# Single indexer heads, and an attention order planned by batches of two groups, in a two-layer streaming encoder

## The chip, the cores and the metric

The kernel runs on one core of a Trainium2 chip. The metric is device time in microseconds (us), the median of three runs. The engines run their own instruction streams and meet at semaphores: TensorE (PE in the rows, with its weight loads as PEld), VectorE (DVE), ScalarE (ACT), GpSimd (POOL) and SyncE (SP), whose queue issues the DMAs. Every engine works through its stream in order.

## The reference, cut to what matters

Two layers over a prompt of 1024 tokens and a sample of 32 tokens that sees a cache of 1024 rows. All arithmetic is in float32.

```python
h = rms_norm(x, g_norm[l]);  a_q, a_k, a_v, i_q, i_k, i_w, b_q, b_k, b_v, m_q, gate = project(h, w_in[l], pos)
# the indexer: 4 heads of 64, one score for every query and key
dots  = einsum('bqhd,bld->bqhl', iq, ik_all)
score = einsum('bqh,bqhl->bql', iw, relu(dots)) * IDX_SCALE      # -inf where the key's chunk is later
_, idx = top_k(score, 256)
# A: softmax attention of 8 heads (2 kv heads) over the chosen keys; B: 4 heads, sliding window, sink;
# M: 4 heads over 256 memory tokens
xp = xp + (concat(o_a, o_b, o_m) * silu(gate)) @ w_out[l]
```

## The kernel before, in words

Tokens are worked in nine tiles: eight of 128 prompt rows (t = 0 to 7) and the sample (t = 8, 32 rows). Tile t has 128 (t + 1) keys, the sample 1056. Keys are not gathered: the top 256 are found as a threshold per query, and a mask in `bias` (0 or -3e38) is added to the scores of group A. Tiles 0 and 1 have at most 256 keys and need no search.

`plan()` writes one list, `STEPS`, and each engine walks it and does its own part of each step. So the list is the order of work on every engine. A layer has these stages:

- **Key stage.** For each tile `SQUARE`, `KEYS` (projection into two score banks), `NORM` (the normed rows of tile t+2 turned by TensorE, copied by VectorE), `KEYS_T` (keys turned), `CACHE` (cache rows turned), `ROPE` (on VectorE). Between them stand the four `INDEX` steps of tile t-2, in the order `KEYS`, INDEX, `NORM`, INDEX, `KEYS_T`, INDEX, `CACHE`, INDEX, `ROPE`. The INDEX steps of tile 7 follow in a row, and those of the sample stand between `QUERIES` 0, `MEM` 0 and `MEM` 1.
- **INDEX before.** `("INDEX", t, hp, c)` is a pair of heads hp and a chunk c of up to 512 keys. TensorE does two matmuls (L837), one head each, on rows 0 to 63 and 64 to 127 of the array. ScalarE does two `Relu` activations (L1053), VectorE a `tensor_scalar` (L1320) or `scalar_tensor_tensor` (L1322) for each head. `index_relu` has two buffers, and step u waits for VectorE to be done with step u-2. A tile has 2 steps up to 512 keys and 4 above, the sample 6.
- **Search.** `TOPK`: 32 rounds on VectorE and ScalarE, beside `QUERIES` and `GATE` on TensorE.
- **Attention.** `attention_steps()` writes it. The items are (t, B), (t, A, kv 0), (t, M), (t, A, kv 1) for each t. `QK` gives scores: an item of kind A takes 2 steps up to 512 keys and 4 above, each a chunk for two heads. VectorE adds the mask, keeps the maximum (L1354) and frees the score buffer. ScalarE then takes the exponentials (L1099) when both chunks are there. For kind B VectorE does the same with the window mask (L1383, exponentials L1113). For kind M (and B of the sample) VectorE only takes the maximum (L1379) and ScalarE reads the score banks itself (L1113), so the banks are held until the exponentials are done.
- `PT` turns a group of four 128x128 blocks of probabilities into one of two `turn_ps` banks (L731). ScalarE (L1124) or VectorE (L1444) copies it to `prob_t`: `copied_by_dve(a)` gives VectorE two groups in five. `PV` multiplies with the values (L915, L927). `MIX` (L1460, VectorE) multiplies with the gate.
- Groups are held until there are two. Then both `PT` are written, then both `PV` of the two groups before. Score steps of item i+2 are dealt out over the groups of item i, each before the `PT` of its group, so ScalarE meets exponentials ahead of the copies of the same pair.
- `OUT` t-1, halves 0 and 1 (L746, 16 instructions each) stand before two groups of tile t (`OUT_AT`). Beside each stands a half of the mask of tile t+1: `need_of_tile` and `mask_tile` (L1210 to L1237). `ADD` (L1474) adds the residual and frees the banks.
- `SCALE` takes the reciprocal of the sums, SP writes it to memory and reads it back spread over partitions (`norm_turn`), and `GATE_SCALE` on GpSimd (L1154) puts it into the gate, which `MIX` waits for. Tile 0 divides its probabilities instead (`DIVIDE`, L1434) before they are turned.

`score_ps` has two buffers of two banks, and `KEYS`, `INDEX`, `QUERIES`, `MEM`, `GATE`, `QK`, `OUT` and `EXTRA` use them by turns. The order around tile 6 before, where each line is one pair of `PT`:

```
QK 6A1.0                 PT 6B.1  PT 6A0.0   PV 5A1.5 MIX PV 6B.0   SCALE 6
OUT 5.0 MASK ADD  QK 6A1.1   PT 6A0.1 PT 6A0.2   PV 6B.1  PV 6A0.0
QK 6A1.2                 PT 6A0.3 PT 6A0.4   PV 6A0.1 PV 6A0.2
```

## Time and profile before

| | |
|---|---|
| median of three runs | 1604.13 us (1602.92 to 1609.43) |
| the profiled execution | 1599.02 us |
| its span | 1597.2 us |
| TensorE's mean granted clock | 0.949 |

The span runs from the first to the last record of the profile. The 1.8 us between it and the profiled execution's time lie around it. Layer 0 takes 0 to 786 us and layer 1 786 to 1566 us, with the same pattern: the attention is 431 to 785 us and 1213 to 1566 us. A row of a timeline gives the start, the duration, the engine, the line, and in brackets how long the engine was idle before it and what ended the wait. Every float32 matmul shows as two instructions.

### The profile page before, as it was taken

Reading aid. Unit: us, or ns where it says so; the run is one execution under the profiler, and the core shown is the slowest. Engines: PE = TensorE matmul, PEld = TensorE weight load, DVE = VectorE, ACT = ScalarE, POOL = GpSimd, SP = SyncE. Lnnn points to the kernel's source line nnn. Section 1 sums busy time; section 2 is a strip of 40 time slices with the busy share of each in tenths; the row PEclk is TensorE's granted clock in tenths of the full one; section 3 lists DMA queues with packets and bytes.
Section 4 is the critical chain, followed back from the end, with each engine's and each line's share of the span. In section 5 each row is a group of like instructions: output and inputs, shape, how many; then the busy total and the mean of one; then the engine's idle time right before and its main releaser. Section 6 shows DMA issues by size and latency. Waiting matters only on the chain. (4 is left out here: it accounts for less than half of the span.)

```text
span 1597.2 us, 19488 instructions
## 1 busy us (share of the span) xinstructions
PE 1400.2 (88%) x6364; PEld 778.1 (49%) x6364; DVE 920.6 (58%) x2527; ACT 657.4 (41%) x1667; POOL 155.9 (10%) x187
## 2 busy tenths in 40 slices
PE   5988799999889999988599887999997999998881
PEld 3444356666545444444344343666664444544450
DVE  1444636887656677655133446488775557676533
ACT  1123526776634433333111334377655333344332
POOL 1100013300001000000011001132000001000003
PEclk9999999999989999999689998999998999999976
DMA  6100410123132312111241004003124222111106
GB/s 200 53 25 21 156 47 1 45 88 94 67 88 73 80 53 54 26 35 29 62 160 52 25 18 161 27 0 119 35 86 133 54 57 57 54 47 53 34 4 247
DMA packets 117960, 108.58 MB, mean 68 GB/s; under 512 B 52368, under 2 KB 90992, under 8 KB 117872
## 3 DMA queue, kind: packets, MB, share of 16 engines
q1 hardware_dynamic: 117872, 107.45, 22.1%
q8 instruction: 51, 0.84, 0.2%
q14 instruction: 37, 0.30, 0.1%
HBM read 81.76 MB, written 25.76 MB: 67 GB/s over the span
## 5 line engine op out<-in xcount | busy, mean ns | idle before, releaser
L746 PE MATMUL score_ps<-w_slot,hT 128*128 128x512 f32 (+2 forms) x1024 | 391.9, 542 | 12.5 <-ACT prob_bm L1053 7.6
L746 PEld LDWEIGHTS score_ps<-w_slot,hT 128*128 128x128 f32 x1024 | 197.7, 196 | 193.3 <-issue 187.3
L746 PE MATMUL score_ps<-w_slot,work 128*128 128x512 f32 x512 | 234.6, 612 | 5.5 <-issue 5.4
L1099 ACT ACTIVATE hT<-hT,neg_top 128x128 f32<-128x128 f32 (+8 forms) x144 | 116.8, 812 | 288.0 <-DVE neg_top L1372 287.8
L1253 DVE TENSOR_SCALAR_CACHE_REDUCE work<-bias,trial 128x384 f32<-128x384 f32 (+3 forms) x256 | 226.1, 883 | 6.9
L969 ACT ACTIVATE work<-bias,neg_trial 128x768 bf16<-128x768 f32 (+2 forms) x192 | 198.4, 1043 | 67.3 <-DVE neg_trial L1249 67.3
L746 PEld LDWEIGHTS score_ps<-w_slot,work 128*128 128x128 f32 x512 | 97.5, 196 | 129.8 <-issue 129.6
L817 PE MATMUL score_ps<-hT,w_slot 128*128 128x352 f32 x448 | 135.2, 460 | 1.4 <-ACT gate_raw L1083 1.4
L731 PE MATMUL turn_ps<-ident,hT 128*128 128x128 f32 (+1 forms) x720 | 98.9, 277 | 27.6 <-ACT work L1124 17.2
L1154 POOL TENSOR_TENSOR work<-work,norm_sb 128x512 f32<-128x512 f32 (+1 forms) x32 | 38.9, 1216 | 855.7 <-DMA norm_sb<-norm_scratch 855.7
L871 PE MATMUL score_ps<-akT,query_mem 64*128 64x512 f32 (+4 forms) x448 | 103.1, 547 | 9.4 <-ACT prob_bm L1113 6.5
L731 PEld LDWEIGHTS turn_ps<-ident,hT 128*128 128x128 f32 (+1 forms) x720 | 74.5, 147 | 74.0 <-issue 33.2
L817 PEld LDWEIGHTS score_ps<-hT,w_slot 128*128 128x128 f32 x448 | 84.8, 190 | 48.4 <-issue 1.7
L1354 DVE CUSTOM_DVE_ANT_0 hT<-score_ps,bias 128x512 f32<-128x512 f32 (+4 forms) x144 | 80.8, 598 | 42.9 <-PE score_ps L871 42.4
L1021 ACT COPY work<-score_ps 128x64 f32<-128x64 f32 (+2 forms) x112 | 20.5, 300 | 179.0 <-PE score_ps L746 179.0
L1124 ACT COPY work<-turn_ps 128x512 f32<-128x512 f32 (+1 forms) x102 | 56.6, 570 | 81.9 <-PE turn_ps L731 81.9
L1474 DVE TENSOR_TENSOR gate_raw<-score_ps,gate_raw 128x512 f32<-128x512 f32 x32 | 22.1, 692 | 118.1 <-PE score_ps L746 118.1
L1320 DVE TENSOR_SCALAR bias<-prob_bm,iw_sign 128x512 f32<-128x512 f32 (+5 forms) x26 | 12.9, 496 | 125.8 <-ACT prob_bm L1053 125.5
L927 PE MATMUL out_a_ps<-work,a_v_sb 128*64 128x256 f32 (+1 forms) x560 | 73.7, 382 | 0.0
L731 PE MATMUL turn_ps<-ident,prob_bm 128*128 128x128 f32 (+2 forms) x280 | 43.3, 286 | 34.3 <-ACT work L1124 24.5
L731 PE MATMUL turn_ps<-ident,work 128*128 128x128 f32 (+1 forms) x284 | 44.3, 292 | 32.8 <-DVE hT L1285 14.9
L1322 DVE SCALAR_TENSOR_TENSOR bias<-prob_bm,iw_sign,bias 128x512 f32<-128x512 f32 (+5 forms) x78 | 51.6, 661 | 29.1 <-ACT prob_bm L1053 26.9
(179 smaller groups left out, 1768.2 us busy)
## 6 DMA issues: line engine op xcount, KB each, us to landing
w_slot<-in_w_in_dram SPq DMA_DIRECT2D x8, 2048.0 KB, 10.3
gate_raw<-in_x_prompt_dram SPq DMA_DIRECT2D x16, 512.0 KB, 3.7
work<-gate_scratch SPq DMA_DIRECT2D x16, 512.0 KB, 4.7
x_scratch<-gate_raw SPq DMA_DIRECT2D x16, 512.0 KB, 4.6
gate_raw<-x_scratch SPq DMA_DIRECT2D x16, 512.0 KB, 3.5
norm_sb<-norm_scratch SPq DMA_DIRECT2D x56, 128.0 KB, 4.1
gate_scratch<-gate_raw SPq DMA_DIRECT2D x16, 264.0 KB, 3.1
gate_scratch<-gate_raw SPq DMA_DIRECT2D x8, 528.0 KB, 2.6
```

The lines of the kernel that those rows point to most:

```text
L731: last = nc.tensor.transpose(flat[0:c, pitch * i:pitch * i + r], src, ident[0:r, 0:r])
L746: last = nc.tensor.matmul(out[:, 0:cols], lhs(k), w[:, k, 0:cols], start=(k == 0), stop=(k == KD - 1))
L817: last = nc.tensor.matmul(o, w[:, k, :], hT_v[:, k, THIRD * c:THIRD * (c + 1)], start=(k == 0), stop=(k == KD - 1))
L871: last = nc.tensor.matmul(out[0:r, 512 * u:512 * u + w], aqT[half, head, t * P:t * P + r], akT[half, k0:k0 + w], start=True, stop=True)
L927: last = nc.tensor.matmul(out[HD * u:HD * (u + 1)], v, p.rearrange("p (h n) -> p h n", h=2), start=first and m == 0, stop=final and m == l ...
L969: ins = nc.scalar.activation(signs[c][0:r, 0:NKEYS[t]], bias[0:r, KEY_OFF[t]:KEY_OFF[t + 1]], ACT.Sign, bias=neg_trial[0:r, i:i + 1], accu ...
L1099: ins = nc.scalar.activation(p, p, ACT.Exp, bias=neg, scale=SM_SCALE, accum_out=sums[t % 2][0:r, col:col + 1])
L1124: nc.scalar.copy(prob_t[a % 4][0:w, 0:n], bank.rearrange("p k n -> p (k n)")[0:w, 0:n]).then_inc(free, 1)
L1154: nc.gpsimd.tensor_tensor(gate_sb[t % 2][:, k, 0:r], gate_sb[t % 2][:, k, 0:r], norm_sb[:, k, 0:r], ALU.mult).then_inc(gate_scaled[bm], 1)
L1253: linked(nc.vector.tensor_scalar(tie_a[0:ROWS[t], 0:NKEYS[t]], scored(c), value[0:ROWS[t], c:c + 1], None, ALU.is_ge, ALU.add, accum_out=c ...
L1322: ins = nc.vector.scalar_tensor_tensor(out=s, in0=rl, scalar=sign, in1=s, op0=ALU.mult, op1=ALU.add)
L1354: ins = nc.vector.tensor_tensor_reduce(prob[0:r, head + at:head + at + w], ps[0:r, 512 * u:512 * u + w], bias[0:r, k0 + at:k0 + at + w], 1 ...
```

## The change

- **Single heads.** `("INDEX", t, h)` is one head over all its keys. TensorE does its chunks one after the other on the same 64 rows of the array, ScalarE one `Relu` over up to 1024 columns, VectorE one operation over all keys. Every tile has 4 steps. The sample's last 32 keys go to `out_bm_ps` with a semaphore of their own, and its relu buffers are `relu_sb`, for which ScalarE waits that the keys are stored. VectorE's own wait for that before the search goes.
- **Batches.** The groups are paired once and for all. Score steps of item i go one to a batch (several where it is crowded), so that the last stands two batches before the item's first `PT`. In a batch stand: `OUT`, parts of the mask, `ADD`, the score steps, both `PT`, the `PV` of the batch before, then the `SCALE` of the scores of the batch before.
- **Copies in front.** ScalarE walks `scalar_order(STEPS)`: exponentials that read SBUF come after the `PT` copies of their batch. Those that read the score banks (M, and B of the sample) stay ahead of the copies.
- **Masks in parts.** The mask of a tile is nine parts; 0 to 2 (only for the tiles of `BY_ACT`: 5, 6 and 7) can stand in batches without an `OUT`, 3 to 5 with or before the first half of `OUT`, 6 to 8 with or before the second.

The new order around tile 6, at the start of the attention and at its end:

```
QK 6A0.3   PT 5A1.3 PT 5A1.4   MIX PV PV
MASK.0     PT 5A1.5 PT 6B.0    MIX PV PV
MASK.1 QK 6A1.0              PT 6B.1  PT 6A0.0   PV 5A1.5 MIX PV 6B.0
OUT 5.0 MASK.2-5 ADD QK 6A1.1    PT 6A0.1 PT 6A0.2   PV PV
QK 6M QK 6A1.2               PT 6A0.3 PT 6A0.4   PV PV
start: EXTRA QK 0A0.0 0A0.1 0M 0A1.0 0A1.1  DIVIDE 0B PT 0B  DIVIDE 0A0 PT 0A0  QK 1B 1A0.0 1A0.1  DIVIDE 0M ...
end:   QK 8M 8A1.0-3  PT 8B.1 PT 8A0.0  PV MIX 7.0 PV / OUT 7.0 ADD  PT PT PV PV SCALE 8.1 SCALE 8.0 / ...
```

```diff
@@ -48,7 +48,6 @@
 SEARCH_STEPS = 32
 
 
...
 CACHE_GROUPS = 6
...
+def batches():
+
+    groups = [(i, g) for i in range(len(ITEMS)) for g in range(len(groups_of(ITEMS[i])))]
+    return [groups[k:k + 2] for k in range(0, len(groups), 2)]
...
+def mask_parts(t):
+
+    return list(range(0 if t in BY_ACT else 3, 9))
...
+def scores_by_batch(first, last):
+
+
+    at, early = [[] for _ in range(last[len(ITEMS) - 1] + 1)], []
+    for i in range(1, len(ITEMS)):
+        units, before = score_steps(i), buffer_of(i)[1]
+        if before is None and first[i] < 2:
+            early += units
+            continue
+        low = 0 if before is None else last[before] + 1
+        for n, unit in enumerate(units):
+            at[max(low, first[i] - 1 - len(units) + n)].append(unit)
+    return early, at
+
+
 def attention_steps():
...
+    plan = batches()
+    first, last = {}, {}
+    for b, groups in enumerate(plan):
+        for i, _ in groups:
+            first.setdefault(i, b)
+            last[i] = b
+    early, scores = scores_by_batch(first, last)
...
+    out, masks = [[] for _ in plan], [[] for _ in plan]
+    for t in range(1, TILES):
+        here, prev = ITEMS.index((t, "B", 0)), ITEMS.index((t - 1, "A", 1))
+        out0 = last[prev] + 2
+        out[out0].append(("OUT", t - 1, 0))
+        if t == SMP:
+            continue
+        ahead = next(b for b in range(len(plan)) if ("QK", ITEMS.index((t + 1, "A", 0)), 0) in scores[b])
+        out1 = max(out0, min(ahead, first[ITEMS.index((t, "M", 0))]))
+        out[out1].append(("OUT", t - 1, 1))
+        if t + 1 in SEARCHED:
+            for k in mask_parts(t + 1):
+                b = first[here] + k if k < 3 else out0 if k < 6 else out1
+                masks[min(b, out0, ahead) if k < 6 else min(b, ahead)].append(("MASK", SEARCHED.index(t + 1), k))
...
+    def products(groups):
+        made = []
+        for i, g in groups:
+            t, kind, kv = ITEMS[i]
+            made.append(("PV", i, g))
+            if g == len(groups_of(ITEMS[i])) - 1 and kind == "M":
+                made.append(("MIX", t, 1))
+            elif g == len(groups_of(ITEMS[i])) - 1 and (kind, kv) == ("A", 1):
+                made.append(("MIX", t, 0))
+        return made
+
+    steps, waiting, mixes = [("EXTRA",)] + early, [], []
+    for b, groups in enumerate(plan):
+        steps += out[b] + masks[b] + [("ADD",) + s[1:] for s in out[b]]
+        steps += scores[b]
+        for i, g in groups:
+            if ITEMS[i][0] == 0 and g == 0:
                 steps.append(("DIVIDE", i))
-            held.append(("PT", i, g))
-            if len(held) == 2 or (i, g) == last_group:
-                steps += held
-                mixes, last_mixes = last_mixes, []
-                steps += mixes
...
+            steps.append(("PT", i, g))
+
+
+        steps += mixes
+        mixes = []
+        for s in products(plan[b - 1]) if b else []:
+            (mixes if s[0] == "MIX" and s[2] else steps).append(s)
+        steps += waiting
+        waiting = [d for q in scores[b] for d in divisors(q)]
+    steps += mixes + waiting + products(plan[-1])
     return steps + [s for t, c in ((NT - 1, 1), (SMP, 0)) for s in (("OUT", t, c), ("ADD", t, c))]
...
+def scalar_order(steps):
+
+
+    order, scores, last = [], [], None
+    for s in steps:
+        if last == "PT" != s[0]:
+            order += scores
+            scores = []
+        if s[0] == "QK" and s[1] and not reads_scores(ITEMS[s[1]]):
+            scores.append(s)
+        else:
+            order.append(s)
+        last = s[0]
+    return order + scores
...
-        index = index_steps(t - 2) if t - 2 in SEARCHED else []
+        index = [("INDEX", t - 2, h) for h in range(IDX_HEADS) if t - 2 in SEARCHED]
...
-    steps += index_steps(NT - 1) + [("KEYS_T", SMP)]
-
-    last = index_steps(SMP)
...
+    steps += [("INDEX", NT - 1, h) for h in range(IDX_HEADS)] + [("KEYS_T", SMP)]
+
     for h, filler in enumerate([("QUERIES", 0), ("MEM", 0), ("MEM", 1)]):
-        steps += [filler] + last[2 * h:2 * h + 2]
-    assert len(last) == 6
+        steps += [filler, ("INDEX", SMP, h)]
+    steps.append(("INDEX", SMP, IDX_HEADS - 1))
...
                         elif kind == "INDEX":
-                            t, hp, c = step[1:]
-                            if (hp, c) == (0, 0):
+                            t, h = step[1:]
+                            if h == 0:
                                 turn_taken(pe, ("KEYS_T", t), 0)
                                 if t == SMP:
                                     turn_taken(pe, ("KEYS_T", t), 1)
-                            r, k0 = ROWS[t], (0 if t < SMP else SEQ) + 512 * c
-                            w = min(512, NKEYS[t] - 512 * c)
+                            r, half, k0 = ROWS[t], HD * (h % 2), 0 if t < SMP else SEQ
                             out = score_buffer(step)
-                            for u in range(2):
-                                half = slice(HD * u, HD * (u + 1))
-                                last = nc.tensor.matmul(out[0:r, 512 * u:512 * u + w],
-                                                        iqT[half, hp, t * P:t * P + r],
-                                                        ikT[half, k0:k0 + w], start=True, stop=True)
+                            q = iqT[half:half + HD, h // 2, t * P:t * P + r]
+                            for c in range(0, NKEYS[t], 512):
+                                w = min(512, NKEYS[t] - c)
+                                if c < 1024:
+                                    o = out[0:r, c:c + w]
+                                else:
+                                    if h:
...
 
                     counted = 0
-                    for step in STEPS:
...
                             nc.scalar.copy(bkT[:, k0:k0 + r], bank[:, 2, 0:r]).then_inc(free, 1)
                         elif kind == "INDEX":
-                            t, hp, c = step[1:]
-                            r, w, u = ROWS[t], min(512, NKEYS[t] - 512 * c), INDEX_STEPS.index(step)
+                            t, h = step[1:]
+                            r, n = ROWS[t], NKEYS[t]
+                            u = IDX_HEADS * SEARCHED.index(t) + h
                             ps, free = scores(step)
                             act.wait_ge(iw_done, t + 1)
+                            relu = (index_relu if t < SMP else relu_sb)[u % 2]
+                            if (t, h) == (SMP, 0):
+                                for b in range(2):
+                                    act.wait_ge(kv_stored[b], 16 * kv_dmas(b, TILES))
                             if u >= 2:
-                                act.wait_ge(score_added, 2 * (u - 1))
-                            for k in range(2):
-                                at = slice(512 * k, 512 * k + w)
-                                ins = nc.scalar.activation(index_relu[u % 2][0:r, at], ps[0:r, at], ACT.Relu,
-                                                           scale=iw_abs[0:r, t, 2 * hp + k:2 * hp + k + 1])
+                                act.wait_ge(score_added, u - 1)
+                            scale = iw_abs[0:r, t, h:h + 1]
+                            ins = nc.scalar.activation(relu[0:r, 0:min(n, 1024)], ps[0:r, 0:min(n, 1024)],
+                                                       ACT.Relu, scale=scale)
                             ins.then_inc(free, 1)
+                            if n > 1024:
+                                ins = nc.scalar.activation(relu[0:r, 1024:n], out_bm_ps[0:r, 0, 0:n - 1024],
+                                                           ACT.Relu, scale=scale)
+                                ins.then_inc(extra_free, 1)
                         elif kind == "QUERIES":
                             t = step[1]
...
 
-                    def need_of_tile(i):
+                    def mask_part(i, k):
...
+                        low, part = least[0:r, i:i + 1], margin[0:r, i:i + 1]
+                        if k == 0:
                             link(nc.vector.tensor_scalar(rank, x, v, None, ALU.is_gt, ALU.add,
                                                          accum_out=count[0:r, i:i + 1]))
+                        elif k == 1:
                             link(nc.vector.tensor_scalar(equal, x, v, 3.4e38, ALU.is_le, ALU.mult))
+                        elif k == 2:
...
                             link(nc.vector.tensor_scalar(part, part, -1.0, 1.0, ALU.mult, ALU.add))
                             link(nc.vector.tensor_tensor(v, v, part, ALU.mult))
                             link(nc.vector.tensor_tensor(v, v, low, ALU.add))
-                        link(nc.vector.tensor_scalar(rank, x, v, None, ALU.is_gt, ALU.add,
-                                                     accum_out=count[0:r, i:i + 1]))
-                        link(nc.vector.tensor_scalar(need[0:r, i:i + 1], count[0:r, i:i + 1], -1.0, float(TOPK),
-                                                     ALU.mult, ALU.add))
-
-                    def mask_tile(i):
...
                             nc.vector.tensor_copy(ikT[:, k0:k0 + r], bank[:, 3, 0:r]).then_inc(free, 1)
                         elif kind == "INDEX":
-                            t, hp, c = step[1:]
-                            r, n, u = ROWS[t], NKEYS[t], INDEX_STEPS.index(step)
-                            w = min(512, n - 512 * c)
-                            scores_taken(dve, step)
-                            s = bias[0:r, KEY_OFF[t] + 512 * c:KEY_OFF[t] + 512 * c + w]
-                            for k in range(2):
-                                rl = index_relu[u % 2][0:r, 512 * k:512 * k + w]
-                                sign = iw_sign[0:r, t, 2 * hp + k:2 * hp + k + 1]
-                                if (hp, k) == (0, 0):
-                                    ins = nc.vector.tensor_scalar(s, rl, sign, None, ALU.mult)
-                                else:
-                                    ins = nc.vector.scalar_tensor_tensor(out=s, in0=rl, scalar=sign, in1=s,
-                                                                         op0=ALU.mult, op1=ALU.add)
-                                signal(ins, score_added, 2 * u + k + 1)
-                            if hp == IDX_HEADS // 2 - 1 and 512 * c + w == n and t < SMP:
-
-                                link(nc.vector.memset(s[0:CHUNK, w - CHUNK:w], NEG))
+                            t, h = step[1:]
+                            r, n = ROWS[t], NKEYS[t]
+                            u = IDX_HEADS * SEARCHED.index(t) + h
+                            if n > 1024:
+                                dve.wait_ge(extra_free, h + 1)
+                            else:
+                                scores_taken(dve, step)
+                            s, rl = bias[0:r, KEY_OFF[t]:KEY_OFF[t] + n], (index_relu if t < SMP else relu_sb)[u % 2][0:r, 0:n]
+                            sign = iw_sign[0:r, t, h:h + 1]
+                            if h == 0:
...
+                            else:
+                                ins = nc.vector.scalar_tensor_tensor(out=s, in0=rl, scalar=sign, in1=s,
...
                         elif kind == "QK":
                             i, j = step[1:]
```

## Rows read from the trace of the kernel before

**Rows 1.** The page: busy time by engine, and the granted clock over 40 slices.

```profile
PE 1400.2 (88%) x6364; PEld 778.1 (49%) x6364; DVE 920.6 (58%) x2527; ACT 657.4 (41%) x1667; POOL 155.9 (10%) x187
...
PEclk9999999999989999999689998999998999999976
```

**Rows 2.** Busy time (count) by engine, clock, DMA by stretch: key stage, attention.

```profile
90.00:208.00 118.00, 97.39 (x375) 47.04 (x374) 57.82 (x123) 39.92 (x116) 4.02 (x8) 0.91 0.22 73
431.00:786.00 355.00, 311.94 (x1768) 165.69 (x1767) 208.41 (x592) 130.35 (x359) 19.87 (x16) 0.95 0.21 56
```

**Rows 3.** Waits by PE, 461 to 745: waiting line, releaser, total, times, longest.

```profile
PE turn_ps L731 <- ACT work L1124: 19.3, 14, 2.5
...
PE turn_ps L731 <- ACT prob_t L1124: 1.9, 2, 0.9
```

**Rows 4.** Busy time of the same stretch.

```profile
461.00:745.00 284.00, 259.60 (x1376) 134.16 (x1375) 181.37 (x479) 106.73 (x286) 18.96 (x14) 0.99 0.19 50
```

**Rows 5.** Timeline, attention, around one wait: start, duration, engine, operation.

```profile
634.63 0.60 PE L731 MATMUL turn_ps<-ident,prob_bm 128*128 128x128 f32 x4
634.67 1.22 DVE L1379 TENSOR_REDUCE top<-score_ps 128x4 f32<-128x1024 f32 x1
...
638.20 0.47 ACT L1113 ACTIVATE prob_bm<-score_ps,neg_top 128x256 f32<-128x256 f32 x1
...
638.65 1.07 ACT L1124 COPY work<-turn_ps 128x512 f32<-128x512 f32 x2
...
639.29 0.66 PE L731 MATMUL turn_ps<-ident,prob_bm 128*128 128x128 f32 x4 [1.99 <-ACT work L1124]
```

**Rows 6.** Timeline, start of attention.

```profile
438.07 0.49 PE L871 MATMUL score_ps<-akT,query_mem 64*128 64x128 f32 x4 [3.27 <-ACT prob_bm L1113]
...
441.46 2.08 PE L884 MATMUL score_ps<-bkT,bqT 64*128 64x256 f32 x8
...
447.02 1.97 PE L731 MATMUL turn_ps<-ident,prob_bm 128*128 128x128 f32 x8 [3.48 <-DVE prob_bm L1434]
```

**Rows 7.** Timeline, key stage, one tile of 512 keys.

```profile
119.89 1.13 PE L837 MATMUL score_ps<-query_mem 64*128 64x512 f32 x4
...
120.95 1.10 PE L731 MATMUL turn_ps<-ident,gate_raw 128*128 128x128 f32 x8
...
122.82 0.49 DVE L1320 TENSOR_SCALAR bias<-prob_bm,iw_sign 128x512 f32<-128x512 f32 x1 [12.86 <-ACT prob_bm L1053]
...
123.34 0.75 DVE L1322 SCALAR_TENSOR_TENSOR bias<-prob_bm,iw_sign,bias 128x512 f32<-128x512 f32 x1
...
124.97 1.05 PE L731 MATMUL turn_ps<-ident,work 128*128 128x128 f32 x7 [1.86 <-DVE hT L1285]
```

**Rows 8.** As rows 2, gaps between projections (INDEX of tiles 2, 3, 4, 5, 6+7, sample).

```profile
97.63:105.93 8.30, 4.75 (x28) 3.10 (x28) 5.37 (x12) 4.17 (x16) 0.00 (x0) 0.91 0.00 0
119.89:128.60 8.71, 4.91 (x28) 2.83 (x28) 5.57 (x12) 4.59 (x16) 0.00 (x0) 0.98 0.00 0
143.17:152.38 9.21, 6.77 (x37) 3.61 (x36) 3.31 (x10) 5.36 (x19) 0.00 (x0) 0.81 0.00 0
165.51:174.27 8.76, 6.19 (x37) 3.23 (x37) 4.32 (x10) 5.63 (x19) 0.00 (x0) 1.00 0.00 0
177.86:198.93 21.07, 12.82 (x59) 5.53 (x56) 17.60 (x37) 11.79 (x29) 0.00 (x0) 0.86 0.77 265
211.62:232.57 20.95, 19.21 (x94) 13.34 (x93) 6.22 (x9) 7.58 (x19) 4.39 (x4) 1.00 0.07 25
```

**Rows 9.** Timeline, PE: the first projection of queries.

```profile
198.93 12.76 PE L746 MATMUL score_ps<-w_slot,hT 128*128 128x512 f32 x32 [3.00 <-ACT prob_bm L1053]
```

**Rows 10.** Timeline: an output projection of 16 instructions.

```profile
523.46 7.10 PE L746 MATMUL score_ps<-w_slot,work 128*128 128x512 f32 x16 [0.41 <-issue]
```

**Rows 11.** Timeline, end of attention: the round trip of the divisors.

```profile
745.16 0.19 DVE L1414 RECIPROCAL inv_sum<-sums 32x8 f32<-32x8 f32 x1
...
753.66 0.45 POOL L1154 TENSOR_TENSOR work<-work,norm_sb 128x128 f32<-128x128 f32 x1 [22.53 <-DMA norm_sb<-norm_scratch]
```

98 lines of the change are left out of this document (30 added, 68 removed).

## The prediction

> **What bounds the kernel now.** The page comes first: TensorE is busy 88% of the span, VectorE 58%, ScalarE 41% [rows 1]. The stretches show where TensorE is not full [rows 2]. In the key stage it works 97.4 of 118 us, in the attention 311.9 of 355, and the granted clock falls to 0.91 and 0.95. VectorE's 208 of 355 and ScalarE's 130 say that neither is full in the attention. So the attention is bound by TensorE's own work plus 43 us a layer in which it waits, and the reader is to ask for whom.
>
> The waits of TensorE from 461 to 745 us give the answer: 19.3 + 1.9 = 21.2 us in 16 waits for ScalarE's copies of turned probabilities [rows 3], of 24.4 us that it idles there (284 - 259.6) [rows 4]. One of them in order of time [rows 5]: TensorE ends its pair of turns at 635.2, VectorE takes the maximum of kind M from 634.67 to 635.9, ScalarE does two exponentials of kind A and four of M until 638.7, and only then the copies, which the next turn awaits for 1.99 us. The copy takes 0.54 us and its data were there 3.4 us before. The exponentials ahead of it are wanted only a batch or more later. What is left of the 43 us lies at both ends of the attention.
>
> **Attention, middle.** The change puts the exponentials of kinds A and B behind the copies. In a batch TensorE does one pair of turns, one pair of products and mostly one score step, some 3.2 us (each about 1.06, as 119.89 to 120.95 for a score pair of 512 columns [rows 7]). After the turns ScalarE copies (0.54 to 1.1 us), then takes two exponentials (about 2.1 to 2.4 us by 1.03 each and the read of the sum), and is free when the next turns end. So most of the 21.2 us go. What stays or is new, worked out from the new order:
> - Kind M still has its four exponentials ahead of the copies: from the end of its matmuls 1.22 + 0.2 on VectorE and 1.9 on ScalarE [rows 5], 3.3 us, then the copy at 3.9, where TensorE (score step, turns, products) has work for 3.2. That is 0.5 to 0.7 us in each of 8 tiles, 5 us.
> - In some batches the score steps are bunched: four before tile 4's second half. VectorE needs some 1.5 us for each, TensorE 1.06 and has two buffers: 1.2 us. Two score steps behind a mask part of 0.6 us hold `MIX` and with it `OUT`: 0.4 us, twice or three times.
> - The mask parts' cost is nothing where they stand beside `OUT`, whose 7.10 us [rows 10] hide 5 to 7 us of mask before and after. Parts 0 and 1 leave it and stand among copies: about 0.3 us, three times.
>
> Together about 6.5 us stay, so 21.2 - 6.5 = 15 us a layer go, between 8 (every bunch hurts and M's wait is 1.5 us) and 20. Removed waits also keep the clock up: it is 0.99 in this stretch [rows 4], so 1% of 284, 2.8 us at half speed, cost 1.4 us; I take 1.
>
> **Attention, start.** Here the order works the other way. Before, `DIVIDE` 0B and the turn of 0B run while TensorE waits 3.27 us for M's exponentials, and the turn of 0A0 comes at 440.4, ahead of 1B at 441.46, and that of 0M at 447.02 [rows 6]. After, TensorE first does 0A1.1 (438.07, unchanged), VectorE then its maxima (0.7) and `DIVIDE` 0B (1.4): turn of 0B at about 440.7. ScalarE copies it (0.6) and only then takes the four exponentials of 0A0 and 0A1, 1.7 us together before the first division can start; `DIVIDE` 0A0 takes 1.1: turn of 0A0 at 445, 4.6 us later than before. Then two score steps more than before (1A0) stand ahead of `DIVIDE` 0M, 1.9 us of VectorE, with 1B's 2.1. The turn of 0M comes at about 452, 5 us late; the steps done early are worth about 1 us again. I book -4.5, and -1 for a longer stay at the low clock (the 2.08 us for the eight instructions at 441.46 are near that level already). Bounds: -8 and -1.
>
> **Attention, end.** All five score steps of the sample now stand ahead of `OUT` 7.0. VectorE has 8 us for them, TensorE 5: it waits some 3 us. In exchange the same waits behind `OUT` go (about 3). `SCALE` 8 comes for both halves at once, behind `OUT` 7.0. One round trip through memory took 745.16 to 753.66, 8.5 us [rows 11], two in a row on SP some 15 us. TensorE has the products and `OUT` 7.1 (7.1 us) for that, about 18 us from the end of `OUT` 7.0 on. So it stays hidden: 0, bounds -3 and +3.
>
> **Key stage.** This is where a gain may be lost. A 512-column float32 matmul takes 7.10 / 8 = 0.89 us in a run of its kind [rows 10], and a pair of INDEX matmuls on the two halves of the array takes 1.06 (119.89 to 120.95) [rows 7]: the pair overlaps. Single heads on one half will not. I price a step at 0.17 + 0.89 n / 512: 0.84 us for 384 keys, 1.06, 1.28, 1.50, 1.73, 1.95 up to 1024, and 2.05 for the sample, times four = 41.6 us. Before, pairs by the same formula per chunk: 1.7, 2.1, 2.9, 3.4, 3.8, 4.2 and 4.7 = 22.8 us. So TensorE gets 18.8 us more work a layer. The other bound is no added work at all, were two matmuls on one half to overlap; nothing shows that.
>
> The Trainium skill speaks against this part too: "TensorEngine Tiling (Array Packing)", Theoretical Speedup, gives up to 2x for a contraction of 64 when both row tiles work. By the rule the single heads would need 2 x 22.8 = 45.6 us where my rows give 41.6. The trace agrees in kind, with 1.06 us for two against 0.89 for one.
>
> But the work falls largely into waits. Between two projections TensorE has 8.3, 8.7, 9.2 and 8.8 us for the steps of 384 to 768 keys, and works 4.8 to 6.8 of them [rows 8]. In the tile of 512 keys the first wait, 1.86 us, is for VectorE's `NORM`, and that stands behind two relus, L1320 and L1322 (0.49 + 0.75) [rows 7]. One relu and one L1320 now stand ahead of it, so the turn comes 1.3 us earlier, 3.8 us after the projection; meanwhile TensorE does 1.06 + 1.03 + 1.06. The second wait, ahead of `CACHE`, is filled by the third INDEX step. Adding up both chains so I get 7.65 us in place of 8.7, and likewise 7.2 for 8.3, 7.9 for 9.2 (there four chunk steps of 128 keys go) and 9.2 for 8.8, where the chain of TensorE is the longer. For tiles 6 and 7 together the gap is 21.1 us, VectorE works 17.6 of it and `QUERIES` 0 waits 3.00 us at its end for a relu that waits for VectorE [rows 8, 9]; half as many, longer operations save VectorE their start-ups, and I book 0.5 us. In the sample's stretch (20.9 us with `MEM`'s matmuls) four steps of 2.05 take the place of six, 4.7 us, and of 1.7 us of waits (20.95 - 19.21): -1.9. Sum: +1.1 + 1.05 + 1.3 - 0.4 + 0.5 - 1.9 = +1.6 us. The clock: 0.91 of 118 us [rows 2] means 21 us at 1.2 GHz, up to 10 us lost. Fuller gaps should win a third back, +3. Key stage: +4.6, bounds -12 and +9. ScalarE's new wait, for the stored keys, has behind it the sample's relus and TensorE's `MEM`; the stores are issued one tile earlier and a projection of 12.8 us lies between, so 0, at most 2.
>
> **Sum.** A layer: 15 + 1 - 5.5 + 0 + 4.6 = 15.1 us; both 30. The profiled execution took 1599.0 (span 1597.2 and 1.8 around), so it becomes 1569. The median of the runs shown is 5 us above it, and I forecast the median: 1604 - 30, **1574 us**.
>
> **The rivals.**
> - *A, the serial heads are exposed (slower).* If the waits of the key stage move with the INDEX steps in place of taking them in, because relu and turn wait for a later matmul, 18.8 us a layer are added. With -5.5 at the start and 15 + 1 in the middle that is -8.3 a layer: 1604 + 17 = 1621. It decides once over 11 of the 18.8 us are exposed (the 16 - 5.5 = 10.5 earned elsewhere). For it: the INDEX matmuls stand in TensorE's own order. Against: 20.6 us of waiting in the stage. 10%.
> - *B, VectorE takes ScalarE's place.* If VectorE's copies, behind score steps, mask parts and `MIX`, now end last, half of the 21.2 us come back: 8.5 + 1 - 5.5 + 2 = 6 a layer, 1592. For it: 181 of 284 us busy, in lumps [rows 4]. Against: it releases hardly any wait now. 17%.
> - *C, the clock stays up and the start is cheap.* 20 + 2 - 3 + 8 = 27 a layer: 1550. For it: TensorE would be idle only some 10 us in the attention. 13%.
> - *D, nothing happens*, because TensorE's own work is all there is: the 21.2 us of waits with a copy in front of each speak against it. Its chance is within B's and the "same" below.
>
> **How the numbers follow.** Forecast 60% (1558 to 1590), A 10%, B 17% (1590 to 1604), C 13% (1540 to 1558). The range that holds 8 in 10 takes in the upper half of C and most of B: 1550 to 1602. Half a percent, 8 us, is about what a measurement can tell from no change. Faster by more (below 1596): 60 + 13 + about 7 of B = 0.80; same 0.10; slower, A, 0.10.
>
> **What would show it.** Right: TensorE's waits for L1124 in the middle fall from 21 to some 5 us a layer, those left stand behind kind M; `OUT` 0.0 starts about 4 us later after the gate stage; L837 takes nearly twice its time, while the key stage gets shorter or stays; its clock rises above 0.91. Wrong: L837's work adds to the gaps between projections (A), TensorE waits for L1444 or L1354 in the middle (B), or `MIX` 8 waits for GpSimd behind `OUT` 7.1's end.

## The result and the profile after

The changed kernel takes 1643.3 us (median of 4 runs, 1642.1 to 1650.2), the kernel before beside it 1605.1. The ratio is 1.025, interval 1.023 to 1.027: 38 us slower, where 1574 was forecast. The profiled execution of after has a span of 1640.6 us and a mean clock of 0.933 (before: 1597.2 and 0.949). Below, one of b_late's three runs (1816.9 us at a mean granted clock of 0.81, where the other two have 0.93) is left out of its median and ratio. The page of after, its busy time and its granted clock, to be read against [rows 1]:

```profile
PE 1441.4 (88%) x6364; PEld 802.2 (49%) x6364; DVE 902.9 (55%) x2479; ACT 654.8 (40%) x1627; POOL 156.1 (10%) x187
...
PEclk9999699999888899999789997999997989999996
```

TensorE is busy 41 us more, and its line of `INDEX` alone accounts for that: 93.8 us (L867) where it was 51.7 (L837). The span is 43 us longer. That invites rival A, that the serial heads are the loss; the stretches say otherwise. The stretches of after that answer to [rows 2] and [rows 4] (key stage, attention, its middle):

```profile
90.00:211.00 121.00, 116.79 (x381) 56.60 (x380) 54.76 (x107) 38.45 (x100) 4.93 (x8) 0.87 0.22 71
434.00:805.00 371.00, 312.81 (x1712) 167.64 (x1715) 206.62 (x591) 130.44 (x359) 18.69 (x16) 0.92 0.20 52
472.00:776.00 304.00, 264.97 (x1384) 137.09 (x1384) 184.43 (x495) 108.69 (x289) 17.78 (x14) 0.95 0.19 47
```

The key stage is 3 us longer and nearly without gaps: 121 - 116.8 = 4.2 us idle, 20.6 before, so the gaps took 16 of its 19 us more work. The attention is the loss: 16 us in this view. For an exact measure I take it from `EXTRA`'s copy to the start of the sample's `OUT`, marks that every kernel has: before 347.2 and 348.3 us (layers 0 and 1), after 369.8 and 367.4. So it is 22.6 and 19.1 us a layer longer. In layer 0, from `EXTRA` to the first `OUT` it takes 30.0 before and 38.6 after, from there to `OUT` 7.0 283.7 and 303.6, from there to the end 33.5 and 27.6: +8.6, +19.9 and -5.9.

TensorE's waits in the middle, to be read against [rows 3]: waiting line, releaser, total, times, longest.

```profile
PE score_ps L770 <- DVE work L1495: 18.2, 3, 7.7
PE score_ps L900 <- ACT prob_bm L1150: 6.2, 6, 3.2
PE score_ps L770 <- issue: 5.9, 3, 2.9
...
PE turn_ps L755 <- ACT work L1161: 0.9, 1, 0.9
```

The waits for ScalarE's copies (L1161, L1124 of before) are gone as intended: 0.9 us in place of 21.2. In their place stand 18.2 + 5.9 = 24.1 us ahead of `OUT` (L770), nearly all of them for `MIX` (L1495). Whom `MIX` awaits is seen in order of time. `SCALE` t.1 makes the reciprocals for kinds B and M of tile t, `SCALE` t.0 those for kind A; `MIX` t.0 comes last and releases `OUT` t.0. Tile 2 in the timeline of after (lines of several engines; SPq is SP's issuing of a transfer):

```profile
519.86 0.20 DVE L1449 RECIPROCAL inv_sum<-sums 128x8 f32<-128x8 f32 x1
...
520.09 0.37 SPq L706 DMA_DIRECT2D norm_scratch<-inv_sum  x1
...
531.19 1.09 SPq L713 DMA_DIRECT2D norm_sb<-norm_scratch  x2
...
532.12 0.19 DVE L1449 RECIPROCAL inv_sum<-sums 128x8 f32<-128x8 f32 x1
...
532.34 0.56 SPq L706 DMA_DIRECT2D norm_scratch<-inv_sum  x1
...
541.46 1.08 SPq L713 DMA_DIRECT2D norm_sb<-norm_scratch  x2
...
546.19 1.26 POOL L1191 TENSOR_TENSOR work<-work,norm_sb 128x512 f32<-128x512 f32 x1 [10.15 <-DMA norm_sb<-norm_scratch]
...
547.54 0.69 DVE L1495 TENSOR_TENSOR work<-out_a_ps,work 128x512 f32<-128x512 f32 x1 [6.86 <-POOL work L1191]
```

and TensorE at its end:

```profile
548.33 9.85 PE L770 MATMUL score_ps<-w_slot,work 128*128 128x512 f32 x16 [7.69 <-DVE work L1495]
```

This is the divisors' round trip, twice. `SCALE` 2.1 makes its reciprocals at 519.9, SP stores them, waits for the store and issues the loads 11.1 us later. `SCALE` 2.0 makes its own at 532.1, just as SP comes free, and theirs is the trip that counts: 9.1 us from the store to the loads, 14.1 from the reciprocals to GpSimd, which scales the gate at 546.2; `MIX` 2.0 has waited 6.9 us, `OUT` 7.7. And `OUT` itself then takes 9.85 us where it took 7.10 [rows 10]: TensorE had been idle and the granted clock of 540 to 560 us is 0.74. In the kernel before, `SCALE` 2.1 ran as `OUT` 1.0 began (491.12) and `SCALE` 2.0 as `OUT` 1.1 began (504.14), not behind it; its store was issued 27.9 us earlier than in after. The gate was then scaled 2.9 us before `MIX` 2.0 began, and `OUT` 2.0 began at 523.46, 24.9 us earlier:

```profile
491.36 0.37 SPq L682 DMA_DIRECT2D norm_scratch<-inv_sum  x1
...
504.20 0.20 DVE L1414 RECIPROCAL inv_sum<-sums 128x8 f32<-128x8 f32 x1
...
504.43 0.37 SPq L682 DMA_DIRECT2D norm_scratch<-inv_sum  x1
...
513.42 1.09 SPq L689 DMA_DIRECT2D norm_sb<-norm_scratch  x2
...
518.51 1.27 POOL L1154 TENSOR_TENSOR work<-work,norm_sb 128x512 f32<-128x512 f32 x1 [10.84 <-DMA norm_sb<-norm_scratch]
...
522.67 0.69 DVE L1460 TENSOR_TENSOR work<-out_a_ps,work 128x512 f32<-128x512 f32 x1 [1.65 <-PE out_a_ps L927]
```

The `OUT`s of the first halves show this in five tiles of layer 0: 6.50, 7.69, 2.94, 4.04 and 2.50 us of wait, 23.7 in all, and matmuls that are 2.95, 2.75 and 1.70 us longer behind the three longest of them: 31 us. In tiles 1, 2 and 4, which have these three, the store of `SCALE` t.0 follows its own reciprocals by 0.2 us, so their late start sets the date; in tiles 3 and 5 it waits another 2 and 1 us for SP, which is still busy with the other half's trip. VectorE's waits for GpSimd at `MIX` are 66.2 us in the whole span (21 times); they were 2.2 (once).

### The profile page after: what moved, and what is told of

It reads as the page before. It is cut to its first block and busy times, and to the rows that moved or that the text cites. A ratio compares the mean times of both kernels' runs of the same rounds, so it can differ in the third digit from the quotient of the medians.

```text
span 1640.6 us, 19412 instructions
## 1 busy us (share of the span) xinstructions
PE 1441.4 (88%) x6364; PEld 802.2 (49%) x6364; DVE 902.9 (55%) x2479; ACT 654.8 (40%) x1627; POOL 156.1 (10%) x187
## 5 line engine op out<-in xcount | busy, mean ns | idle before, releaser
L770 PE MATMUL score_ps<-w_slot,hT 128*128 128x512 f32 (+2 forms) x1024 | 387.4, 537 | 5.7 <-DMA w_slot<-in_w_in_dram 5.4
L770 PE MATMUL score_ps<-w_slot,work 128*128 128x512 f32 x512 | 246.5, 638 | 52.9 <-DVE work L1495 30.6
L770 PEld LDWEIGHTS score_ps<-w_slot,hT 128*128 128x128 f32 x1024 | 195.7, 194 | 185.4 <-issue 179.3
L770 PEld LDWEIGHTS score_ps<-w_slot,work 128*128 128x128 f32 x512 | 102.1, 205 | 183.9 <-issue 183.7
L1161 ACT COPY work<-turn_ps 128x512 f32<-128x512 f32 (+1 forms) x102 | 57.9, 576 | 258.3 <-PE turn_ps L755 258.1
L755 PE MATMUL turn_ps<-ident,hT 128*128 128x128 f32 (+1 forms) x720 | 95.0, 273 | 14.8 <-DVE hT L1469 11.9
L867 PE MATMUL score_ps<-query_mem 64*128 64x512 f32 (+2 forms) x192 | 93.8, 675 | 0.3 <-ACT prob_bm L1086 0.3
L900 PEld LDWEIGHTS score_ps<-akT,query_mem 64*128 64x128 f32 (+1 forms) x448 | 35.6, 181 | 67.3 <-ACT prob_bm L1150 25.1
L1150 ACT ACTIVATE prob_bm<-score_ps,neg_top 128x256 f32<-128x256 f32 (+2 forms) x80 | 36.0, 460 | 67.2 <-DVE neg_top L1430 66.9
L1086 ACT ACTIVATE prob_bm<-score_ps,iw_abs 128x384 f32<-128x384 f32 (+5 forms) x48 | 41.5, 864 | 47.8 <-PE score_ps L867 44.3
```

The lines of the kernel that those rows point to most:

```text
L755: last = nc.tensor.transpose(flat[0:c, pitch * i:pitch * i + r], src, ident[0:r, 0:r])
L770: last = nc.tensor.matmul(out[:, 0:cols], lhs(k), w[:, k, 0:cols], start=(k == 0), stop=(k == KD - 1))
L867: last = nc.tensor.matmul(o, q, ikT[half:half + HD, k0 + c:k0 + c + w], start=True, stop=True)
L900: last = nc.tensor.matmul(out[0:r, 512 * u:512 * u + w], aqT[half, head, t * P:t * P + r], akT[half, k0:k0 + w], start=True, stop=True)
L1086: ins = nc.scalar.activation(relu[0:r, 0:min(n, 1024)], ps[0:r, 0:min(n, 1024)], ACT.Relu, scale=scale)
L1161: nc.scalar.copy(prob_t[a % 4][0:w, 0:n], bank.rearrange("p k n -> p (k n)")[0:w, 0:n]).then_inc(free, 1)
```

## The experiments

The kernel before was measured again beside each group of runs (medians of 1606.1, 1610.5, 1607.9 and 1607.1 us), so ratios are compared. The attention's length is from `EXTRA` to the sample's `OUT` as above.

| kernel | median us | ratio to before, interval | attention, layers 0 and 1 |
|---|---|---|---|
| before | 1606.1 | 1 | 347.2, 348.3 |
| after | 1643.3 | 1.0252 (1.0232 to 1.0271) | 369.8, 367.4 |
| a_early | 1587.1 | 0.9899 (0.9860 to 0.9938) | 338.6, 341.1 |
| a_nonorm | 1588.1 | 0.9896 (0.9859 to 0.9934) | 340.0, 342.6 |
| after_rowstore | 1584.9 | 0.9857 (0.9822 to 0.9892) | 337.4, 339.3 |
| b_order | 1606.1 | 0.9993 (0.9972 to 1.0014) | 352.0, 348.6 |
| b_single | 1610.3 | 1.0038 (1.0008 to 1.0067) | 353.7, 348.1 |
| a_early_exps | 1617.6 | 1.0044 (1.0013 to 1.0074) | 352.7, 353.1 |
| b_late | 1676.0 | 1.0409 (1.0333 to 1.0484) | 382.7, 382.3 |
| a_early_pairs | 1589.4 | 0.9869 (0.9817 to 0.9922) | 341.1, 340.6 |
| a_early_start | 1581.0 | 0.9812 (0.9760 to 0.9864) | 336.0, 335.8 |
| a_start_mask | 1579.3 | 0.9821 (0.9791 to 0.9851) | 335.7, 335.9 |
| a_start_mask_spread | 1584.3 | 0.9839 (0.9810 to 0.9868) | 337.1, 340.1 |

**The divisors a batch earlier** (a_early).

```diff
-    steps, waiting, mixes = [("EXTRA",)] + early, [], []
+    steps, mixes = [("EXTRA",)] + early, []
...
-        steps += waiting
-        waiting = [d for q in scores[b] for d in divisors(q)]
-    steps += mixes + waiting + products(plan[-1])
+        steps += [d for q in scores[b] for d in divisors(q)]
+    steps += mixes + products(plan[-1])
```

> The changed kernel with one thing moved: SCALE and GATE_SCALE stand at the end of the batch whose score steps complete the sums, not a batch later, so that the reciprocals of tile t kinds B and M come before OUT t-1 half 0 again. Theory 1 (MIX is held by the divisors' round trip through memory, which begins a batch and an OUT too late): TensorE's waits ahead of OUT (18.2 us for MIX and 7.2 us of issue in layer 0) fall under 5 us, the low clock behind them goes, the time falls by 2 x 20 to 2 x 28 us to 1587 to 1603. Rival (MIX is held because the two round trips of a tile run in series on SP's queue whatever their start, or by the mask parts): the waits ahead of OUT stay over 15 us a layer and the time stays over 1630.

It fell to 1587: 56 us from one batch. (`SCALE` t.0 is thereby ahead of `OUT` t-1.1 again in every tile. `SCALE` t.1 is ahead of `OUT` t-1.0 only up to tile 3: in tiles 4 to 7 the new plan has kind M's own score step behind that `OUT`.) The middle of its attention, 468 to 745 us of the profiled execution, waits and busy time:

```profile
PE score_ps L769 <- issue: 6.1, 5, 2.0
PE score_ps L899 <- ACT prob_bm L1149: 5.9, 6, 2.6
...
PE score_ps L769 <- DVE work L1494: 0.8, 1, 0.8
```

```profile
468.00:745.00 277.00, 259.40 (x1385) 135.57 (x1386) 186.64 (x496) 109.77 (x291) 18.10 (x14) 0.99 0.20 51
```

No wait of `MIX` for GpSimd is left, and the clock is at 0.99, as in [rows 4]. In tile 2 both halves' stores are now issued at 496.9 and 508.5, each inside an `OUT` of 7.1 us, and `OUT` 2.0 waits 0.8 us. What remains ahead of `OUT`, 6.1 + 0.8 us, is no wait for GpSimd. No run moves only one of the two `SCALE`s; that `SCALE` t.0 is the one that counts is read from the trace of after, and from t.1 staying late here in four tiles at no cost.

**No round trip at all** (a_nonorm).

```diff
-                        norm_turn(t, 1)
-                        norm_turn(t, 0)
...
-                            pool.wait_ge(norm_loaded[bm], 32 * t)
...
-                                                    norm_sb[:, k, 0:r], ALU.mult).then_inc(gate_scaled[bm], 1)
+                                                    gate_sb[t % 2][:, k, 0:r], ALU.mult).then_inc(gate_scaled[bm], 1)
...
-                            if t >= 3:
-                                dve.wait_ge(norm_written[bm], 16 * (t - 2))
```

> The changed kernel without the round trip of the divisors: SP neither stores nor loads them, GpSimd multiplies the gate by itself in place of by the divisors, so the heads' outputs aren't divided; all other work stands. Theory 1: the price of the whole round trip in this order is what is gained, at least what a_early gains: 1580 to 1600, with no wait of VectorE's MIX for GpSimd over 1 us. Rival (serial INDEX heads or kind M's score banks are the loss): under 15 us gained, over 1628.

1588, the same as a_early within the intervals (0.4%). So a_early gained all that this measurement can find in the round trip: a batch earlier, it is hidden.

**A cheaper store, everything else as in the changed kernel** (after_rowstore). The transfers of after by median us from issue to landing (line, count, KB each) show which term of the trip is long:

```profile
norm_sb<-norm_scratch SPq DMA_DIRECT2D x56, 128.0 KB, 4.1
...
norm_scratch<-inv_sum SPq DMA_DIRECT2D x28, 4.0 KB, 9.0
```

The store of 4 KB takes over twice the load of 128 KB. It writes 1024 single numbers, since each head's stand in a row of their own.

```diff
-                            sp.dma_start(rows.rearrange("c q -> q c"), inv_sum[t % 2][0:r, 8 * bm:8 * bm + 8]
+                            sp.dma_start(norm_dram[t % 2, bm].rearrange("c q -> (c q)").rearrange(
+                                "(q c) -> q c", c=8)[0:r], inv_sum[t % 2][0:r, 8 * bm:8 * bm + 8]
```

> The changed kernel with the divisors' late start left in, but each row's eight reciprocals stored side by side in memory (128 pieces of 32 bytes) in place of each head's in a row of its own (1024 single numbers of 4 bytes). The load is unchanged and so reads them in another order: the divisors reach the wrong heads and queries, all work stands. The store now lands 9.0 us after its issue (median of 28). Theory 1 (the scattering is what costs, and it is the longest term of the chain): landing 2 to 4 us, two stores a tile save 10 to 14 us of the chain, so the waits ahead of OUT fall under 8 us a layer and most of the 56 us that a_early gained come back: 1585 to 1605. Rival (the 9 us are the fixed cost of a store whose receipt is waited for): landing stays over 7 us, time over 1630.

The same two lines of after_rowstore:

```profile
norm_sb<-norm_scratch SPq DMA_DIRECT2D x56, 128.0 KB, 2.9
...
norm_scratch<-inv_sum SPq DMA_DIRECT2D x28, 4.0 KB, 1.4
```

The store lands in 1.4 us and the kernel takes 1585, with `SCALE` as late as in after. So the loss needs both, the late start and the 9 us of the store; either one mended brings it all back. The divisors reach the wrong heads in this kernel; what a load that sorts them would take was not run.

**The same delay in the kernel before** (b_late).

```diff
-    steps, late, waiting, held, last_mixes = [], [], [], [], []
+    steps, late, waiting, held, last_mixes, ready = [], [], [], [], [], []
...
             if g == 0:
-                steps += waiting
-                waiting.clear()
+                steps += ready
+                ready, waiting = waiting, []
             waiting += made
```

> The kernel before with nothing changed but the divisors: SCALE and GATE_SCALE of each half come one item later (for kinds B and M of tile t behind OUT t-1 half 0, as in the kernel after). Theory 1 (this delay is what the change lost by): waits of TensorE ahead of OUT of 15 to 25 us a layer and a lower clock behind them, 1605 + 30 to 55 = 1635 to 1660. Rival (the loss needs the new plan's score order too): under 1620.

1676 (two runs), 4.1% slower than before, more than expected (1635 to 1660), probably since here the delay is an item and not a batch. The waits have the same place, ahead of `OUT`; the copies wait much as before (41.7 there). Waits of TensorE over the whole span:

```profile
PE score_ps L746 <- issue: 49.9, 12, 9.5
PE turn_ps L731 <- ACT work L1124: 46.0, 30, 3.5
```

This shows the cause without any other part of the change: the old plan too has less slack for the divisors' start than one item.

**Copies in front, alone** (b_order).

```diff
-                    for step in STEPS:
+                    for step in scalar_order(STEPS):
```

(with the changed kernel's function, its condition `s[1]` replaced by `ITEMS[s[1]][0]`, so that tile 0 keeps its order)

> The kernel before with one part of the change: on ScalarE alone the copies of turned probabilities go in front of the exponentials of kinds A and B (tile 0 keeps its order). Plan, masks, index pairs as before. Theory 1 (the copies in front were right and worth what the prediction said): waits of TensorE for the copies fall from 23 us a layer to under 7, time 1605 - 2 x 13 to 17 = 1571 to 1579. Rival (the copies' waits come back as waits for exponentials or for VectorE, so that this part is worth nothing): 1598 to 1608.

Nothing was gained: 0.9993. The rival was right. The waits of TensorE in the middle (462 to 749 us) show where they went; the second view is one of them in order of time:

```profile
PE turn_ps L747 <- ACT hT L1115: 10.0, 7, 2.4
PE turn_ps L747 <- ACT work L1140: 9.5, 6, 2.5
```

```profile
604.92 0.60 ACT L1140 COPY work<-turn_ps 128x512 f32<-128x512 f32 x1
...
605.38 0.96 ACT L1115 ACTIVATE hT<-hT,neg_top 128x768 f32<-128x768 f32 x1
606.32 0.95 ACT L1115 ACTIVATE hT<-hT,neg_top 128x768 f32<-128x768 f32 x1
...
607.40 0.66 PE L747 MATMUL turn_ps<-ident,hT 128*128 128x128 f32 x4 [2.40 <-ACT hT L1115]
```

The exponentials (L1115) that were put behind the copy are those of the next turns. In the old plan the score steps stand so late that an item's last exponential is due at once: the queue only changed what is late. From the first `OUT` to `OUT` 7.0 TensorE idles 19.2 of 284.2 us (24.4 of 284 in [rows 4]), and what that saves goes in the clock, 0.96 where it was 0.99.

**Early scores, alone** (a_early_exps, against a_early).

```diff
-                    for step in scalar_order(STEPS):
+                    for step in STEPS:
```

> a_early with ScalarE in the plan's own order again, its exponentials in front of the copies (scores still two batches ahead). In the kernel before the copies in front alone moved the wait from the copies to the exponentials (11.9 us behind L1115, nothing gained). Theory 1 (the two parts need each other: early scores make the exponentials wait-able, copies in front use that): without the copies in front TensorE waits for copies again, 15 to 22 us a layer, 1587 + 30 to 44 = 1617 to 1631. Rival (the early scores alone are enough, since the exponentials are then done before the turns end): 1583 to 1598.

1618, ratio 1.0044: TensorE waits for the copies again, 14.3 + 2.1 = 16.4 us in the middle (468 to 755 us):

```profile
PE turn_ps L754 <- ACT work L1160: 14.3, 12, 3.2
...
PE turn_ps L754 <- ACT prob_t L1160: 2.1, 3, 1.3
```

So the copies in front are worth 1.45% (1.0044 to 0.9899) with early scores and nothing (0.9993) without. That the early scores alone are no gain can be said less surely: in 1.0044 stand the single heads (0.4% in b_single) and the new start too.

**Single heads, alone, and pairs in the new attention** (b_single, a_early_pairs). b_single is the changed kernel with the old `attention_steps`, the old two places of the mask and ScalarE in plan order; a_early_pairs is a_early with the old `INDEX` steps.

> The kernel before with one other part of the change: single indexer heads (and the wait for the stored keys on ScalarE); attention's plan, order and masks as before (a mask's parts together in their two old places). Theory 1 (the serial heads are hidden in the waits between projections, as the trace of after reads: +2.9 us in layer 0, -1.0 in layer 1): 1603 to 1610. Rival A of the prediction (heads exposed): 1621 to 1642.

> a_early with the kernel before's indexer: pairs of heads on both halves of the array, chunks of 512 keys. By b_single the single heads cost 4 us (0.38%, interval 0.08 to 0.67): theory 1 expects 1581 to 1586, rival (the single heads are worth something beside the new attention, by the clock) 1588 to 1595.

Single heads cost 0.4% in the old kernel. In the new one the ratios are 0.9899 and 0.9869 with intervals that overlap, so that they are worth no more there; which is better isn't settled. Rival A is out. The same 80 matmuls of the stage take 41.4 us in layer 0 of after and 21.4 before, and the stage grows by 3:

```profile
L867 PE MATMUL score_ps<-query_mem 64*128 64x512 f32 (+3 forms) x80 | 41.4, 706 | 0.0
```

```profile
L837 PE MATMUL score_ps<-query_mem 64*128 64x512 f32 (+3 forms) x80 | 21.4, 615 | 0.8 <-ACT prob_bm L1053 0.7
```

**Tile 0 in the old order** (a_early_start, against a_early).

```diff
-    steps, mixes = [("EXTRA",)] + early, []
+    steps, mixes = [("EXTRA",)] + early + [("DIVIDE", 0)], []
...
-        steps += scores[b]
+        steps += scores[b] + ([("DIVIDE", 1)] if b == 0 else [])
...
-            if ITEMS[i][0] == 0 and g == 0:
+            if ITEMS[i][0] == 0 and g == 0 and i > 1:
...
-        if s[0] == "QK" and s[1] and not reads_scores(ITEMS[s[1]]):
+        if s[0] == "QK" and ITEMS[s[1]][0] and not reads_scores(ITEMS[s[1]]):
```

> a_early with tile 0 as in the kernel before: DIVIDE of 0B ahead of the last scores of 0A1, DIVIDE 0A0 ahead of both turns, and tile 0's exponentials not moved behind copies. The prediction booked 5.5 us a layer for the new start; the trace of after shows 8.5 (30.0 to 38.55 up to OUT 0 half 0, in which some score work of 2 us is done earlier). Theory 1: 5 to 7 us a layer come back, 1573 to 1579. Rival (the start's chain is hidden by what follows): 1583 to 1590.

From `EXTRA` to the first `OUT` it takes 34.1 us in layer 0 in place of a_early's 37.9 (34.1 and 38.8 in layer 1), the whole attention is 2.6 and 5.3 us shorter. The time, 1581 at 0.9812, agrees with that, though its interval still touches a_early's; the expected 5 to 7 us a layer were too many. The start of the changed kernel, TensorE's turns and what they wait for, in the kernel after:

```profile
440.61 0.49 PE L900 MATMUL score_ps<-akT,query_mem 64*128 64x128 f32 x4 [3.27 <-ACT prob_bm L1150]
443.22 1.12 PE L755 MATMUL turn_ps<-ident,prob_bm 128*128 128x128 f32 x4 [2.12 <-DVE prob_bm L1469]
447.73 1.12 PE L755 MATMUL turn_ps<-ident,hT 128*128 128x128 f32 x4 [3.39 <-DVE hT L1469]
...
456.14 1.97 PE L755 MATMUL turn_ps<-ident,prob_bm 128*128 128x128 f32 x8 [3.02 <-DVE prob_bm L1469]
464.49 0.66 PE L755 MATMUL turn_ps<-ident,hT 128*128 128x128 f32 x4 [2.57 <-DVE hT L1469]
```

a_early_start has the first of these divisions' waits (2.12) not at all and the second at 0.81; the last two stay.

**Mask parts and the sample's scores** (a_start_mask, against a_early_start, and a_start_mask_spread, against a_start_mask).

```diff
-                b = first[here] + k if k < 3 else out0 if k < 6 else out1
-                masks[min(b, out0, ahead) if k < 6 else min(b, ahead)].append(("MASK", SEARCHED.index(t + 1), k))
+                masks[out0 if k < 6 else out1].append(("MASK", SEARCHED.index(t + 1), k))
```

```diff
-            at[max(low, first[i] - 1 - len(units) + n)].append(unit)
+            late = int(n > 0 and i == len(ITEMS) - 1)
+            at[max(low, first[i] - 1 - len(units) + n) + late].append(unit)
```

> a_early_start with the mask parts 0, 1 and 2 put beside OUT half 0 with parts 3, 4 and 5, in place of one batch each before it. In a_early_start VectorE does part 1 (0.7 to 1.1 us) ahead of the score steps that stand before the MIX of OUT 3.0, and TensorE waits 2.3 us there, 1.4 ahead of OUT 2.0, 0.8 ahead of OUT 4.0. Theory 1 (prediction's bound of 0.3 us, three times, for parts 0 and 1 was too low): 1 to 2 us a layer come back, ratio to the kernel before 0.002 below a_early_start's. Rival: no difference, or the longer mask beside OUT holds the next scores and costs 1 to 3 us a layer.

> a_start_mask with the last three of the five score steps that the change puts ahead of OUT 7.0 moved behind it, as in the kernel before. In a_early TensorE waits there 1.04 and 2.59 us for kind M's exponentials in the score bank and 1.4 for MIX. Theory 1 (the bunch costs what its waits show, and the steps hide behind OUT 7.0): 2 to 4 us a layer. Rival (as the prediction booked it: the waits only change places, 0).

Both make no difference that can be told: 0.9821 and 0.9839 beside 0.9812. Spread scores take TensorE's waits for kind M's banks from 18.1 to 12.9 us (whole span), and the attention isn't shorter (337.1 and 340.1 us for 335.7 and 335.9). The best time measured is a_start_mask's, 1579 us, 1.8% under the kernel before; a_early_start can't be told from it.

## Why the prediction was wrong

**The step that failed: `SCALE` in the middle.** The prediction followed `SCALE` 8 at the end of the sample, gave the round trip its 8.5 us [rows 11] and two in a row 15, and found them hidden. In its sum for the middle the divisors have no term: it never asked the same of tiles 1 to 7, though the change moves `SCALE` t.0 from ahead of `OUT` t-1.1 to behind it in all of them (and `SCALE` t.1 from ahead of `OUT` t-1.0 to behind it in tiles 2 to 7). Between `SCALE` 2.0 and `MIX` 2.0 stand three batches after the change, 3 x 3.2 = 9.6 us by its own numbers, where `OUT` 1.1 and four batches stood. A trip of 8.5 us and the scaling of the gate would have looked just about hidden there: so the size was wrong too. 8.5 us, from the reciprocals to GpSimd, was the trip of the sample's 32 rows. With 128 rows it is 14.1 us, and 15.4 pass until `MIX` 2.0, 5.8 more than the three batches; `OUT` 2.0 waits 7.7. The trace of before had the size, 14.3 us from 504.20 on, and the slack: the gate was ready 1.9, 2.9, 4.4 and 7.3 us before `MIX` t.0 in tiles 1 to 4, and `SCALE` t.0 was moved behind an `OUT` of 7.1 us. The list of what it would be wrong by names "`MIX` 8 waits for GpSimd", the right wait in the wrong tile. What it cost: 56 us (after to a_early, medians), and 31 us in layer 0 of the trace.

**The copies' 15 us a layer: right, and by more luck than reason.** The terms that stay add up to about 8 us (5 + 1.2 + 1 + 0.9) and not to the 6.5 that were taken off, so by its own list the prediction had 13; and a clock of 0.99 over 284 us costs 2.8 us by the way that it reckons the key stage, not 1.4. a_early is the change without the fault. Its middle is 8.0 us shorter than before (275.7 against 283.7), though three score steps of the sample, 4.5 us of matmuls and the 2.6 us that they wait, were moved into it from behind `OUT` 7.0: without them -15.1. But the prediction gave the gain to the copies' new place alone; b_order shows nothing for that. It has ScalarE "free when the next turns end" and calls the exponentials "wanted only a batch or more later". That holds only for the new plan's scores.

**What stays: right in size, at another place.** Forecast were 0.5 to 0.7 us in each of 8 tiles behind kind M. In a_early TensorE waits 0.55 to 0.60 us in four tiles of layer 0, but its score step waits for the bank that M's exponentials read (L899 for L1149), not a turn for a copy. The mask's parts, booked at 0.3 us three times, and the bunches at 1.2 can't be told from zero.

**The start: sign right, too small.** +5.5 was booked; the stretch to the first `OUT` grew by 8.6 in layer 0 and 8.0 in layer 1, with one score step of about 1 us done earlier in it. "`OUT` 0.0 starts about 4 us later": it started 8.6 later after the `EXTRA` copy. Counted from there the turn of 0B comes 2.2 us and that of 0A0 4.8 us later than before, as worked out; that of 0M comes 6.6 later (5 were booked), and another 2.0 are lost between it and `OUT` 0.0, where the turn of 0A1 waits 2.57 us for its division. The order of tile 0 explains 3.9 and 4.7 of it (a_early_start).

**The end: right.** From `OUT` 7.0 on it is 5.9 us shorter, but three score steps, 4.5 us of matmuls and 3.2 of wait, now stand ahead of it: 1.8 longer together, where 0 was forecast with bounds of 3. The sample's `OUT` waits 1.4 us for the two trips.

**The key stage: the work right, the clock wrong.** Single heads were priced at 41.6 us a layer, pairs at 22.8; they take 46.9 and 25.9 (half of 93.8 and 51.7). At the full clock the price holds: a step of tile 6 was put at 1.73 us and takes 1.77; much of the rest is low clock (3.35 for the same step, below). The gaps took the work as worked out. In the tile of 512 keys TensorE waits 0.52 us ahead of `NORM`'s turn (1.86 in [rows 7]), in after:

```profile
120.95 1.05 PE L755 MATMUL turn_ps<-ident,work 128*128 128x128 f32 x7 [0.52 <-DVE hT L1321]
```

But the 3 us for a better clock turned into a loss: the clock of the stage fell from 0.91 to 0.87, in one place (below). Up to the attention layer 0 is 2.5 us slower and layer 1 0.8 faster, where 4.6 faster was forecast.

**The sum.** The forecast for the profiled execution was 1569. Without the late divisors (a_early) it is 1583.5 + 1.8 = 1585.3, so 16 us are missing. The attention gained 8.6 and 7.2 us of the 10.5 forecast a layer: 5 us missing. From the sample's `OUT` or the beginning to `EXTRA` the key and gate stages gained 0.6 us in layer 0 and lost 2.9 in layer 1, of +4.6 each: 11.5 missing. The remaining 57 us of the profiled spans, 1640.6 - 1583.5, are the divisors.

## What to carry to other kernels

When a plan moves a step, follow every moved step to its consumer in every tile, shortest first, and above all a step that starts a transfer: here 4 KB that go to memory and back set the date of the whole tile, and in the profile of before TensorE never waits for them, because they are hidden until the start slips. What can be read there is the slack, the time from when the step's result is ready to when its consumer begins: 1.9 us in tile 1, against a step moved behind 7.1. A trip is measured on a full tile, not on the smallest, and its dearest term may be mended where it stands: the store by pieces in place of single numbers gave as much as the better order (with the load not yet made to fit). Two edits can be worth nothing alone and 1.5% together, so a price taken from the waits of one trace belongs to the pair. A queue reordered without earlier input only renames what is late.
